# Strip buffers and arena moved to SBUF addresses that are multiples of 512 bytes, in a two-layer decoder trunk with expert retrieval

## The reference, cut to what matters

```
act = gelu(einsum('td,thkd->thk', xb, u_tab[eid]))
return einsum('thk,thkd->td', gate * act, v_tab[eid])
```

## The kernel before, in words

| buffer | start | modulo 512 |
|---|---|---|
| ident | 16,512 | 128 |
| pair_ones, ones, masks, early, causal_ts | 17,024 to 24,704 | 128 |
| pars | 26,304 | 192 |
| xres | 26,944 | 320 |
| xT | 35,136 | 320 |
| ln_par | 43,328 | 320 |
| wring | 51,680 | 480 |
| arena | 76,256 | 480 |
| mrows | 221,664 | 480 |

## Time and profile before

### The profile page before, as it was taken

One profiled execution on the slowest core, in us unless ns is written; L12 is line 12 of the kernel. 1 busy time (PEld: TensorE's weight loads), 2 busy tenths in 40 slices (PEclk: granted clock), 3 DMA queues, 4 the chain that ended last, 5 costly groups with the idle time before them and its releaser, 6 DMA issues.

```text
span 1804.5 us, 18617 instructions
## 1 busy us (share of the span) xinstructions
PE 1544.5 (86%) x6020; PEld 925.0 (51%) x6020; DVE 1063.3 (59%) x2499; ACT 604.9 (34%) x1759; POOL 579.8 (32%) x561
## 2 busy tenths in 40 slices
PE   8999998898777778998899978998999968777776
PEld 7779887754222225763456525763457523222222
DVE  1583543577888865334555447665555568864444
ACT  1434311233333333227532323336632333332222
POOL 2000000334443442333433432334432434444331
PEclk9999858999999999999999999998999999999999
DMA  6222003899999999999999999999999999999996
GB/s 246 95 92 72 1 11 130 342 390 419 419 420 419 420 420 413 419 419 420 419 415 419 414 420 416 420 419 420 419 378 419 405 420 421 419 420 420 420 419 260
DMA packets 92063, 638.32 MB, mean 354 GB/s; under 512 B 11072, under 2 KB 13120, under 8 KB 15424
## 3 DMA queue, kind: packets, MB, share of 16 engines
q0 software_dynamic: 73728, 536.90, 72.0%
q1 hardware_dynamic: 18240, 100.24, 14.3%
HBM read 636.05 MB, written 1.05 MB: 353 GB/s over the span
## 4 chain that ended last, share of the span: by engine, by line
PE 49%; DMA 37%; DVE 6%; ACT 5%; issue 2%; POOL 1%; ACTq 0%; SPq 0%; POOLq 0%; DVEq 0%
DMA arena<-l_peer_uv,arena 34%; PE psum L906 21%; PE psum L588 14%; PE psum L887 4%; DVE arena L1716 3%; DMA wring<-l_w_in 2%; PE psum L765 1%; DMA wring<-l_peer_wq 1%; PE psum L681 1%; PE psum L810 1%; PE psum L671 1%; PE psum L680 1%; ACT L1203 1%; POOL arena L555 1%; ACT early L1216 1%
## 5 line engine op out<-in xcount | busy, mean ns | idle before, releaser
L555 POOL DMA_INDIRECT arena<-l_peer_uv,arena x512 | 566.7, 1107 | 1112.0 <-PE psum L906 851.4
L1716 DVE CUSTOM_DVE_ANT_0 arena<-arena,xres 128x1024 f32<-128x1024 f32 x512 | 620.1, 1223 | 437.8 <-DMA arena<-l_peer_uv,arena 436.4
L906 PE MATMUL psum<-arena,early 128*128 128x512 f32 x1024 | 477.8, 611 | 105.8 <-ACT early L1216 105.8
L906 PE MATMUL psum<-arena 128*128 128x512 f32 x1024 | 476.4, 610 | 106.9 <-ACT arena L1216 106.8
L906 PEld LDWEIGHTS psum<-arena 128*128 128x128 f32 x1024 | 189.8, 193 | 367.9 <-issue 205.6
L906 PEld LDWEIGHTS psum<-arena,early 128*128 128x128 f32 x1024 | 189.4, 193 | 365.4 <-issue 194.6
L588 PE MATMUL psum<-xT,wring 128*128 128x128 f32 (+2 forms) x1856 | 296.5, 320 | 13.6 <-DMA wring<-l_w_in 8.4
L588 PEld LDWEIGHTS psum<-xT,wring 128*128 128x128 f32 (+1 forms) x1856 | 269.2, 192 | 52.5 <-issue 21.0
L1203 ACT ACTIVATE arena<-arena 128x2 f32<-128x2 f32 x256 | 52.1, 203 | 628.4 <-DVE arena L1716 628.2
L1031 ACT COPY arena<-psum 128x256 f32<-128x256 f32 (+2 forms) x138 | 62.5, 471 | 222.6 <-PE psum L588 125.8
L1208 ACT ACTIVATE arena<-arena 128x1 f32<-128x1 f32 x512 | 123.3, 287 | 23.8
(11 more groups left out here) (236 smaller groups left out, 1149.5 us busy)
## 6 DMA issues: line engine op xcount, KB each, us to landing
wring<-l_w_in SPq DMA_DIRECT2D x47, 1024.0 KB, 9.4
wring<-l_peer_wq SPq DMA_DIRECT2D x24, 1024.0 KB, 9.3
wring<-l_w_out SPq DMA_DIRECT2D x12, 1024.0 KB, 11.3
arena<-l_peer_uv,arena POOLq DMA_INDIRECT x512, 17.8
ln_par<-l_ln_g SPq DMA_DIRECT2D x6, 512.0 KB, 12.4
ln_par<-l_ln_b SPq DMA_DIRECT2D x6, 512.0 KB, 15.6
arena<-l_peer_keys SPq DMA_DIRECT2D x2, 1024.0 KB, 7.0
xT<-x_t SPq DMA_DIRECT2D x1, 1024.0 KB, 5.0
```

Of the source, the lines that this page charges most:

```text
L555: pool.indirect_dma_start(out=ring[:, g % RING, :], out_offset=None, in_=T[f"l{l}_peer_uv"], in_offset=bass.IndirectOffsetOnAxis(ap=eid[:, ...
L906: last = mm(self.ps[c], diag[k % DIAGS], ring[:, g % RING, D + c * 512:D + (c + 1) * 512], start=not self.begun, stop=True, skip_group_che ...
L1716: v.tensor_tensor_reduce(out=u, in0=u, in1=xres[:, self.b, :], scale=1.0, scalar=0.0, op0=ALU.mult, op1=ALU.add, accum_out=hid[:, self.b, ...
```

## The change

Eight small buffers (`iota16`, `one_mu`, `kn8`, `cexp`, `lnst`, `lnmv`, `lnrs`, `dcol`) are declared first, then `wring` and `arena`, then all others in their old order. No instruction, shape, semaphore, queue or order of work is changed, only addresses in SBUF. The total is the same 211,712 bytes.

```diff
+        iota16 = sb("iota16", [P, TOPK])
+        one_mu = sb("one_mu", [P, RWKV_COLS // P])
+        kn8 = sb("kn8", [P, 8])
+        cexp = sb("cexp", [P, 6])
+        lnst = sb("lnst", [P, NB, 12])
+        lnmv = sb("lnmv", [P, NB, 2])
+        lnrs = sb("lnrs", [P, NB])
+        dcol = sb("dcol", [P, 8])
+        wring = sb("wring", [P, WRING, KT, STRIP])
+        ARENA = 36352
+        A = sb("arena", [P, ARENA])
         ident = sb("ident", [P, P])
...
-        iota16 = sb("iota16", [P, TOPK])
         pars = sb("pars", [P, P])
-        one_mu = sb("one_mu", [P, RWKV_COLS // P])
-        kn8 = sb("kn8", [P, 8])
...
-        cexp = sb("cexp", [P, 6])
...
-        lnst = sb("lnst", [P, NB, 12])
-        lnmv = sb("lnmv", [P, NB, 2])
-        lnrs = sb("lnrs", [P, NB])
-        wring = sb("wring", [P, WRING, KT, STRIP])
-        ARENA = 36352
-        A = sb("arena", [P, ARENA])
-
...
-        dcol = sb("dcol", [P, 8])
```

## The result

The changed kernel took 1779.18 us (median of 4 runs, 1777.73 to 1783.83) against 1805.94 us of the kernel before beside it: ratio 0.9855, 95% interval 0.983 to 0.988. That is 26.8 us between the medians, and 1.45% less by the ratio. The forecast was no change, with a range that went down to 1788 us.

A forecast was written before the change was run, and what follows sets the result against it. The prediction took DMA to lead in most of the time from 330 us on. All terms were zero, so the 1804.5 us span plus 2.15 us around it gave 1806.65 us; forecast 1806.8 us, range 1788 to 1813 us.

The forecast's parts named there:

- What bounds the kernel: Whole kernel: shortening a gather's packets is worth something in most of the 1474.5 us from 330 us on.
- Packets of a DMA: Gather, strip and first-load packets: no change in duration; bounds 14 ns shorter to 4 ns longer, of 316 ns.
- TensorE, ScalarE, GpSimd and VectorE: Matmuls, diagonals, gather issue and dots: zero change; bounds 2 ns a matmul either way, 0 to +61 ns a dot.
- Rival B: VectorE dots: two streams at one remainder collide, 1.08 us more a dot, 71 us in all, 1878 us; chance 0.03.
- Rival C: Gather packets get 4 ns longer, 1.3%, costing 19 us: 1826 us; chance 0.05.
- Rival A: DMA packets get shorter by 4 ns, 2.2% or 4.4%: 1788, 1776 or 1746 us; chance 0.11.
- The sum: Whole kernel: 1804.5 us span plus 0, with 2.15 us around it, 1806.65 us; forecast 1806.8 us.

The follow-up runs named there:

- e4 to e7: The changed kernel with pads ahead of the strips, putting strips, arena and all behind at 256, 64, 128, 32 modulo 512: 1781.24, 1800.90, 1799.36, 1803.44 us.
- e8: The changed kernel with the five odd ring slots moved on by 128 bytes, so every second gather starts off a multiple of 256: 1780.50 us, ratio 0.9876.
- e1: The changed kernel with a 480-byte pad ahead of the strips, putting strips, arena and all behind at 480 modulo 512: 1804.96 us, ratio 0.9997.
- e9: The kernel before with a 32-byte pad ahead of the arena, putting it at 0 modulo 512, strips still at 480: 1780.72 us, ratio 0.9877.
- e12: The changed kernel with ring slots 0 to 4 at 0 and slots 5 to 9 at 128 modulo 256: 1782.48 us, ratio 0.9869.

## Why the prediction was wrong, point by point

**What bounds the kernel** stood: DMA leads from 330 us to the end, and 25.2 of the 26.8 us came between the first gather and the last.

**Packets of a DMA: this step failed.** It bounded the saving by 14 ns and chose zero. Measured are 316 - 311 = 5 ns of a gather's packet (5.7 before rounding), or 1.63% more packets in equal time. The choice rested on one pair, `xT` at 320 and a strip at 480 in 5.0 and 5.1 us, "the pair that differs in nothing but its remainder". Both remainders are off a multiple of 256, 64 and 224 past one, and the series of e4 to e7 shows that all such starts cost about the same. The pair compared off with off; the row that was wanted, off against on, was not in the trace, and so the rows could not carry the choice. Moreover the first loads show little of the cost: those at 4 to 9 us take 312 ns both before and after, and only the ones at 15 to 18 us have come down, from 163 to 160 ns. Means of the saturated stretch and of the first loads stood beside each other, 316 against 312, and I put those 4 ns down to the queue of the gathers, since both write at 480. The changed kernel has gathers at 311, below the 312 of the first loads; the difference was nearly all the start address, at work only where DMA stays full of such packets. The trace of before did hold both prices for one remainder, in the durations of its packets. The second strip has 309 ns and the third, behind it in the same queue and at 480 too, 318 (309 after the change); the first three gathers have 309 to 310 ns and the next ones 314 and more. Packets of one queue and one remainder that differ by more than the 4 ns were the sign that the queue's kind need not be what makes them.

The Trainium skill's rule ("DMA: Bandwidth & Descriptors", section "How a descriptor splits into AXI transactions") names a boundary of 256 bytes, and the runs agree about that: 0 and 256 are free, 32, 64, 128 and 480 are not. They disagree about its size. By an estimate from its beats, starts 32, 64, 128 and 224 bytes past a boundary would cost 0.4, 0.8, 1.6 and 2.7% of an 8192-byte row; the windows lost 1.6, 1.3, 1.3 and 1.6%, and nothing while every second gather was off. The page tells it of reads, and here the written side moved. Where a rule names the very boundary that a change moves across and no row lies on the other side of it, a small difference between rows that are all off is no ground for a chance of 0.11.

**TensorE, ScalarE, GpSimd and VectorE** stood: the groups that the prediction priced are within 2 ns of before, GpSimd's issue within 7, and the dot with both streams at 0 takes 1223 ns. Rival B's collision does not exist at these addresses. Rival C has the wrong sign.

**Rival A** was the case that came: shorter packets and a shorter time. Its sizes were 1788, 1776 and 1746 us. With the measured 5.7 ns of 316.4 (1.8%) its own working gives 0.018 x 1474.5 = 26.5 us, less 1.0 us where TensorE leads in 1095 to 1200 us, so 1807 - 25.5 = 1781.5 us, and 1779.2 us were measured. The model of what a shorter packet is worth came out within 3 us, and the range, cut at its smallest size, did not hold. Its mechanism, as the prediction put it, has each packet that is off pay by itself; e8 shows that it does not.

**The sum** of the other terms, zero, was right: with the remainder given back by padding (e1) the new order of declarations is worth nothing that can be told (ratio 0.9997, 0.9983 to 1.0012).

## What to carry to other kernels

Where DMA bounds a stretch, work out the address of each destination in SBUF modulo 256: a large buffer behind a few small ones can be off by 32 bytes, and one pad of 32 bytes (e9) was worth 1.2% of this kernel (0.9 to 1.5%). Look first at the buffer that takes most of the packets. Here the strips, a small part of the traffic, needed nothing once the gathers were on a multiple, and cost up to 5 us while these were off. And before like is compared with like in a trace, see whether both rows lie on the same side of the boundary in question, and in a stretch where the queue has been full for some time.

## What was not expected of the hardware

- A start off a multiple of 256 bytes costs 5 ns of an 8192-byte packet with all gathers off, nearly the same for 32, 64, 128 and 480: 11,529 to 11,568 packets where 11,717 are done in 200 us. The read side was not tried: no run changed the tables in HBM or how they are declared.
- The same start is free when every second gather has it (11,718 packets), and free for strips among gathers that are on a multiple (14,143 packets in 700 to 940 us, 14,142 without it).
- It is free, too, for the first three gathers of a stretch (309 to 310 ns in the kernel before, then 314 and more), and for three to four that follow five gathers on a multiple (e12).
- A product of two streams at the same remainder, 0 and 0, on VectorE takes 1223 ns, as at 480 and 320.
